# Gated linear attention inside a two-block model: the gate product in one visit on three row quarters, the state products two token tiles at a time

## The reference, cut to what matters

```
gq, gk, gv, gr, glr, fq, fk, fv, ff = split(xn @ w_in[i])
log_a = log_sigmoid(glr @ w_alpha_up[i] + b_alpha[i]) / 16   # glr: (L, 16), log_a: (L, 256)
# chunks: 16 meta tokens, then 8 chunks of 64 tokens
log_b = cumsum(log_a) within a chunk
u_c   = sum_s (k_s * exp(log_end - log_b_s)) v_s^T           # per head 64 x 128
S_c   = exp(log_end_c) * S_{c-1} + u_c
o_t   = q_t^T S_c
```

## Time and profile before

| | us |
|---|---|
| median of 3 runs | 2226.08 (2225.97 to 2226.41) |
| the profiled execution | 2226.62 |
| its span, first to last instruction | 2225.4 |
| PE busy | 2203.2 (99%) |
| DVE, ACT, POOL busy | 1410.5, 1049.4, 119.3 |

### The profile page before, as it was taken

One profiled execution on the slowest core, in us unless ns is written; L12 is line 12 of the kernel. 1 busy time (PEld: TensorE's weight loads), 2 busy tenths in 40 slices (PEclk: granted clock), 3 DMA queues, 4 the chain that ended last, 5 costly groups with the idle time before them and its releaser, 6 DMA issues.

```text
span 2225.4 us, 39293 instructions
## 1 busy us (share of the span) xinstructions
PE 2203.2 (99%) x15807; PEld 2019.1 (91%) x15807; DVE 1410.5 (63%) x2601; ACT 1049.4 (47%) x1947; POOL 119.3 (5%) x203
## 2 busy tenths in 40 slices
PE   9999999999999999999999999999999999999998
PEld 7799999999997899999899888978899888998997
DVE  5356676759743466767689566869455465863664
ACT  5356544347533466543377443223244444552652
POOL 3000010000000001100000010101000000000001
PEclk9999999999999999999999999999999999999999
DMA  6655677345434446642365272768721122543651
GB/s 215 171 128 150 184 185 201 102 143 176 135 93 128 116 131 149 180 118 89 121 173 163 91 180 83 194 176 222 205 72 65 63 97 89 156 159 117 183 170 51
DMA packets 97112, 313.01 MB, mean 141 GB/s; under 512 B 13810, under 2 KB 17812, under 8 KB 95908
## 3 DMA queue, kind: packets, MB, share of 16 engines
q1 hardware_dynamic: 84628, 220.93, 30.8%
q0 software_dynamic: 11584, 88.25, 17.4%
q10 hardware_dynamic: 720, 1.31, 0.2%
HBM read 308.32 MB, written 86.02 MB: 177 GB/s over the span
## 4 chain that ended last, share of the span: by engine, by line
PE 93%; DVE 4%; ACT 2%; issue 1%; DMA 0%; POOL 0%; SPq 0%; ACTq 0%; DVEq 0%; POOLq 0%
PE G L1452 58%; PE G L1489 15%; PE G L1568 7%; PE X L1489 3%; PE X L1788 1%; PE X L1875 1%; PE X L1740 1%; PE X L1764 1%; DVE wL L2465 1%; ACT wH L1928 1%; PE X L1859 1%; PE X L1528 1%; PE X L1844 1%; PE X L1452 1%; PE X L1831 0%
## 5 line engine op out<-in xcount | busy, mean ns | idle before, releaser
L1928 ACT ACTIVATE wH<-raw 128x512 fp32r<-128x512 f32 (+3 forms) x693 | 475.0, 705 | 459.6 <-PE G L1452 381.1
L2465 DVE TENSOR_TENSOR wL<-raw,wH 128x512 fp32r<-128x512 f32 (+3 forms) x693 | 537.8, 788 | 216.4 <-ACT wH L1928 213.5
L1452 PE MATMUL G<-aH,wH 128*128 128x264 f32 (+2 forms) x2000 | 497.2, 314 | 2.4 <-DVE aL L2478 1.7
L1452 PE MATMUL G<-aH,wL 128*128 128x264 f32 (+2 forms) x2000 | 478.9, 305 | 0.0
L1452 PE MATMUL G<-aL,wH 128*128 128x264 f32 (+2 forms) x2000 | 478.8, 304 | 0.0
L1452 PEld LDWEIGHTS G<-aH,wH 128*128 128x128 f32 x2000 | 324.2, 188 | 22.3 <-DVE aL L2478 2.1
L1452 PEld LDWEIGHTS G<-aH,wL 128*128 128x128 f32 x2000 | 322.4, 188 | 16.2
L1452 PEld LDWEIGHTS G<-aL,wH 128*128 128x128 f32 x2000 | 322.7, 188 | 13.1 <-issue 0.2
L1489 PE MATMUL G<-seven,wH 128*128 128x256 f32 (+2 forms) x960 | 177.4, 284 | 1.8 <-DVE wL L2465 1.7
L2624 DVE TENSOR_TENSOR hT<-G,hT 128x528 f32<-128x528 f32 (+1 forms) x83 | 58.0, 699 | 170.3 <-PE G L1452 170.1
L1489 PEld LDWEIGHTS G<-seven,wH 128*128 128x128 f32 x960 | 148.2, 189 | 3.9 <-issue 3.0
(11 more groups left out here) (412 smaller groups left out, 3898.7 us busy)
## 6 DMA issues: line engine op xcount, KB each, us to landing
raw<-weights SPq DMA_DIRECT2D x195, 512.0 KB, 4.1
weight_sums<-weights POOLq DMA_DIRECT2D x72, 704.0 KB, 6.5
raw<-weight_sums SPq DMA_DIRECT2D x160, 256.0 KB, 2.9
raw<-weights SPq DMA_DIRECT2D x48, 704.0 KB, 4.2
raw<-weights SPq DMA_DIRECT2D x121, 256.0 KB, 2.9
weight_sums<-weight_sums POOLq DMA_DIRECT2D x24, 704.0 KB, 5.2
weight_sums<-weights POOLq DMA_DIRECT2D x24, 448.0 KB, 5.1
raw<-weights SPq DMA_DIRECT2D x12, 384.0 KB, 7.5
```

The lines of the kernel that those rows point to most:

```text
L1452: done = e.matmul(m.pair(i)[0:M, bank, 0:n], a[:, k, 0:M], b[:, kx, lo - t0:lo - t0 + n], start=(k == 0 and c == 0), stop=(k == nk - 1 and ...
L1928: e.activation(m.high(i)[:, c], m.raw(i)[:, c], ACT.Copy).then_inc(s.w_hi, 1)
L2465: e.tensor_tensor(m.low(i)[:, c], m.raw(i)[:, c], m.high(i)[:, c].bitcast(F32), ALU.subtract).then_inc(s.w_lo, 1)
```

## The change

The gate product of all five token tiles is made in one step `gz`, and the ACT and DVE chains that used to stand in the three `gz` steps are now three steps `gla` at the old places. For this the low-rank rows exist three times, in row quarters 32, 64 and 96 of `glrT`, and so do the weights `wau`: `sel` has 112 columns, DVE scales three copies, POOL fills ones in rows 32 to 127, and SP issues three loads in place of one. Block 0 uses quarter 96, block 1 quarter 32, block 2 quarter 64; the meta block is computed 128 tokens wide. The state increments are made for token tiles 0 and 1, 2 and 3, and 4, in three visits; two tiles share a bank, side by side. The visits are three background steps apart in place of two.

```diff
             step("fsum", l)
             yield
+            step("gz", l)
             for bk in range(3):
-                step("gz", l, bk)
+                step("gla", l, bk)
                 yield
...
-            for c in range(5):
+            for c in (0, 2, 4):
                 step("gst", l, c)
+                yield
                 yield
                 yield
...
-        self.sel = sb("sel", [128, 48])
+        self.sel = sb("sel", [128, 112])
...
-            self.glrT = sb("glrT", [64, L], F32, c)
+            self.glrT = sb("glrT", [128, L], F32, c)
...
-                self.wau = sb("wau", [49, 256], F32, cf)
+                self.wau = sb("wau", [113, 256], F32, cf)
...
-            done = e.matmul(m.pair(i)[0:48, bank, 0:n], m.sel[:, :], m.osq[:, lo:lo + n], start=True, stop=True)
+            done = e.matmul(m.pair(i)[0:112, bank, 0:n], m.sel[:, :], m.osq[:, lo:lo + n], start=True, stop=True)
...
-    def gz(l, bk):
-        if bk == 0:
-            e.wait_ge(s.psum, NTH["evac", AT["gq", l, 1]])
-            e.wait_ge(s.alpha, 16 * (l + 1))
-        if bk == 2:
-            e.wait_ge(s.rtok, RTOK["attn", l])
-        mt = TOK[BLOCKS[bk][0]][1]
-        for q, j in enumerate(BLOCKS[bk]):
-            t0 = TOK[j][0]
-            done = e.matmul(X[0:mt, bk, 256 * q:256 * q + 256], m.glrT[32:49, t0:t0 + mt], m.wau[32:49, :],
+    def gz(l):
+
+        e.wait_ge(s.psum, NTH["evac", AT["gq", l, 1]])
+        e.wait_ge(s.alpha, 48 * (l + 1))
+        e.wait_ge(s.rtok, RTOK["attn", l])
+        e.wait_ge(s.kzero, l + 1)
+        for bk, q in (0, 0), (1, 0), (2, 0), (1, 1), (2, 1):
+            t0, g = TOK[BLOCKS[bk][q]][0], (96, 32, 64)[bk]
+            done = e.matmul(X[:, bk, 256 * q:256 * q + 256], m.glrT[g:g + 17, t0:t0 + 128], m.wau[g:g + 17, :],
                             start=True, stop=True)
-        done.then_inc(s.gz, 1)
+            if q == len(BLOCKS[bk]) - 1:
+                done.then_inc(s.gz, 1)
...
-        e.wait_ge(s.kd, 3 * l + (1 if c == 0 else 2 if c < 3 else 3))
-        for pr in range(2):
...
+        e.wait_ge(s.kd, 3 * l + (2 if c < 2 else 3))
+        for d in range(c, min(c + 2, 5)):
+            for pr in range(2):
+                for hh in range(2):
+                    q = slice(64 * hh, 64 * hh + 64)
+                    for hf in range(2 if d else 1):
+                        r, at = slice(64 * hf, 64 * hf + 64) if d else slice(0, 16), 256 * (d % 2) + 128 * pr
+                        done = e.matmul(X[q, hf, at:at + 128], m.gk[r, d, 128 * pr + 64 * hh:128 * pr + 64 * hh + 64],
+                                        m.gv[r, d, 256 * pr + 128 * hh:256 * pr + 128 * hh + 128], start=True, stop=True)
...
             scaled(i, m.ffT[:, :], slice(0, 8)).then_inc(*own.one())
-            scaled(i, m.glrT[32:48, :], slice(32, 48)).then_inc(s.psum, 1)
+            for g in (32, 64):
+                scaled(i, m.glrT[g:g + 16, :], slice(g, g + 16)).then_inc(*own.one())
+            scaled(i, m.glrT[96:112, :], slice(96, 112)).then_inc(s.psum, 1)
...
     def gst(l, c):
-        e.wait_ge(s.gst, 18 * l + (4 * c + 2 if c else 2))
+        end = min(c + 2, 5)
+        e.wait_ge(s.gst, 18 * l + 4 * end - 2)
+        for d in range(c, end):
+            state(l, d)
...
         constant(m.glrT[32:64, :], 1.0)
+        constant(m.glrT[64:128, :], 1.0)
...
-        for c, n, row in (0, 8, 0), (32, 16, 8):
+        for c, n, row in (0, 8, 0), (32, 16, 8), (64, 16, 8), (96, 16, 8):
...
-    e.dma_start(m.wau[32:49, :], WAU[0]).then_inc(s.alpha, 16)
+    for g in (32, 64, 96):
+        e.dma_start(m.wau[g:g + 17, :], WAU[0]).then_inc(s.alpha, 16)
```

More of the change, by code:

```diff
@@ L1670, in gst @@
             e.wait_ge(s.state, 9 * l + 2 * c - 1)
-        e.wait_ge(s.kd, 3 * l + (1 if c == 0 else 2 if c < 3 else 3))
-        for pr in range(2):
[L1673 to L1680, removed]
+        e.wait_ge(s.kd, 3 * l + (2 if c < 2 else 3))
[7 more added lines that the diff above has]
+                                        m.gv[r, d, 256 * pr + 128 * hh:256 * pr + 128 * hh + 128], start=True, stop=True)
+                        if pr:
+                            done.then_inc(s.gst, 1)
     def go(l, v):
@@ L2262, in attin, with gla @@
         operand_high(m.q2H[:, h, :] if h < 2 else m.aH[:, h, NM:L], m.attnT[:, h, :], 1.0)
-    def gz(l, bk):
+    def gla(l, bk):
         n = 3 * l + bk + 1
@@ L2400, in act_program @@
     parts = {"high7": high7, "p1st": p1st, "p5th": p5th, "u2nd": u2nd, "c21": c21, "conv7": conv7, "silu7": silu7, "hidh7": hidh7, "split": split, "prep": prep, "xm": xm, "gains": gains, "ffc": ffc, "sq": sq, "rms": rms, "prepmid": prepmid, "last": last, "rmshalf": rmshalf, "rmsmid": rmsmid, "rmsend": rmsend, "midln": midln, "midexp": midexp,
-             "tmout": tmout, "rest": rest, "evac": evac, "mixin": mixin, "attin": attin, "gz": gz, "gb": gb, "gdec": gdec,
+             "tmout": tmout, "rest": rest, "evac": evac, "mixin": mixin, "attin": attin, "gla": gla, "gb": gb, "gdec": gdec,
              "go": go, "gn": gn, "fsum": fsum, "ft": ft, "fs": fs, "fo": fo, "nsq": nsq, "nsum": nsum, "is": iscore, "dt": dt,
@@ L2905, in gst, with state @@
     def gst(l, c):
-        e.wait_ge(s.gst, 18 * l + (4 * c + 2 if c else 2))
+        end = min(c + 2, 5)
+        e.wait_ge(s.gst, 18 * l + 4 * end - 2)
+        for d in range(c, end):
+            state(l, d)
+    def state(l, c):
         if c == 0:
@@ L2917, in gst @@
                 done = e.scalar_tensor_tensor(out=m.S[:, n, pr, :], in0=m.S[:, n - 1, pr, :], scalar=m.dec[:, pr, n - 1:n],
-                                              in1=X[:, hf, 128 * pr:128 * pr + 128], op0=ALU.mult, op1=ALU.add)
+                                              in1=X[:, hf, 256 * (c % 2) + 128 * pr:256 * (c % 2) + 128 * pr + 128],
+                                              op0=ALU.mult, op1=ALU.add)
                 if pr:
@@ L3077, in dve_program @@
              "rmsmid": rmsmid, "midln": midln, "rtok": rtok, "tmout": tmout, "evac": evac, "rest": rest, "normed": normed, "last": last, "store": store,
-             "pads": pads, "gz": gz, "gb": gb, "gst": gst, "gn": gn, "fsum": fsum, "fs": fs, "fmeta": fmeta, "fn": fn, "ftail": ftail,
+             "pads": pads, "gla": gla, "gb": gb, "gst": gst, "gn": gn, "fsum": fsum, "fs": fs, "fmeta": fmeta, "fn": fn, "ftail": ftail,
              "iw": iw, "is": iscore, "itri": itri, "top": top, "mask": mask, "dt": dt, "ds": ds, "dn": dn}
@@ L3207, in pool_program @@
                                    compare_op=ALU.not_equal, fill=1.0, base=-row, pattern=[[-1, n]], channel_multiplier=1)
-            if (t, c) == (3, 32):
+            if (t, c) == (3, 96):
                 done.then_inc(s.sel, 1)
@@ L3247, in zeros @@
             e.wait_ge(s.chunk, AT["seven", 0, 1, 10, 4] + 1)
-            e.dma_start(m.wau[32:49, :], WAU[1]).then_inc(s.alpha, 16)
+            for g in (32, 64, 96):
+                e.dma_start(m.wau[g:g + 17, :], WAU[1]).then_inc(s.alpha, 16)
     def store(half, j):
```

## The result

The changed kernel takes 2222.26 us (median of 20 runs, 2221.86 to 2222.85), the kernel before 2226.22 in the same rounds (20 runs, 2225.83 to 2227.50). The ratio is 0.9982, with a 95% interval of 0.9977 to 0.9988: 3.96 us or 0.18% less, where 4.9 us and 0.22% were forecast. The time lies in the stated range of 2220.1 to 2224.0, but above the forecast's own range of 2220.4 to 2221.7, at the place of rival (b). The gain is within 0.2%: the prediction gave that a chance of 0.34, and 0.62 to more than 0.2%.

What follows compares the result with a forecast made beforehand. PE, busy for 99% of the span, was taken to bound the kernel. Savings of 2 x (1.77 + 0.36 + 0.32) = 4.9 us off the median of 2226.08 gave 2221.2, 0.22% faster, with a range of 2220.1 to 2224.0.

Steps and rivals of the forecast that it cites:

- rival (b): Quarters run at once, but a just-in-time hand-over fails or `ffsel` keeps its price: 0.5 to 2 us lost; chance 0.25.
- Part 1, the gate product: Three `gz` visits (3.05 us) become one of five matmuls on three row quarters (1.28): gain 1.77 a layer.
- (a): In the gate product the quarters run one after another: gain only 2.2 us, time 2223.8; chance 0.08.
- (c): In the gate product each change of quarter empties the array: 4.05 against 3.05 us, time 2226.7; chance 0.03.
- Part 2, the state products: Five state visits (3.78 us a layer) become three (3.42): gain 0.36 a layer.
- the bound without it: First state visit with no change of tiling counted: the added set costs 0.44, not 0.60, gain 0.52 a layer.
- Part 3, the selector: At 112 columns `ffsel` no longer runs in a 64-column tile: gain 0.32 a layer, 0 if still a tile.
- Part 4: Work added elsewhere, DVE copies, POOL selects and memset, SP issues: all taken as covered and priced at 0.
- The other thin hand-over, the bank at 40.5: Layer 0: the bank for the first `gv` product is emptied at 40.5, PE reaches it at 40.8; priced at 0.
- Rival (d): The merge does nothing, because something taken as covered, such as `kzero`, now sets PE's time; chance 0.02.
- first of its two signs of being wrong: The prediction is wrong if the attention stages together give back less than 4.4 us.
- the second: The prediction is wrong if a stage without any edit changes its length.

Runs made afterwards that it cites:

- beside: The changed kernel with the gate product and two of the three state visits moved directly behind meta rows: 2221.03 us (0.9978).
- states: The kernel before with only the state visits merged, three in place of five: 2225.66 us (0.9997).
- wide: The kernel before with only the selector widened to 112 columns, the added ones zero: 2225.53 us (0.9997).
- serial: The changed kernel with all five gate products on one row quarter, the other copies still made and loaded: 2225.57 us (0.9996).

## Why the prediction was right in its mechanism and 0.94 short

**Part 1, the gate product: right.** The visit has 1.07 for a forecast of "about 1.08", and layer 1 gained 1.77, to the hundredth. That is a product of concurrency, as assumed: 2.35 on one quarter, near the 2.41 of its upper bound (2.61 without the 0.20). Rivals (a) and (c) are out: neither 2.4 nor 4 was seen. The 0.20 for leaving the whole array and coming back is confirmed from another side by `beside`, at 0.26 for each adjacency. That it is the array's tiling which is left and come back to is the reading of these rows; what they show is the time.

**Part 2, the state products: mis-sized.** The sum gave 0.36 a layer; the traces give 0.26 and 0.23, and `states` by itself 0.58 for both layers. The visits' own rows are as forecast (1.18, 1.03 and 0.60), and with 1.18 in the first visit the change from 16-row to 64-row tiles did cost like a set of its own (0.58 + 0.60). This is the case with a drain at a change of tiling mode, as the Trainium skill has it (TensorEngine Tiling (Array Packing), Key Properties), and not the bound without it. What was mis-sized is the block behind: the sum took 0.228 a product and 0.20 over for every block. By the same measure the blocks behind the visits of 1.18 and 1.03 have 0.23 over (4.33 and 7.07), and the one behind the meta rows at 76.64, which had a visit directly behind them in the kernel before and now stand alone, has 0.25 (2.99). The row for that was there: in the kernel before, the chain behind the meta rows that stand alone at 92.21 reads

```profile
93.21 2.99 PE G L1568 x12
```

Together 0.03 + 0.03 + 0.05 = 0.11, the missing 0.1 of a layer. What all three have in common is the pace of 0.231 to 0.232 for 10 or 11 products and not 6; DVE's reads are not in it.

**Part 3, the selector: right**, at 0.32 a layer, and `wide` shows that 112 columns are treated as the whole array.

**Part 4, priced at 0: wrong twice, by little.** The split ended at 35.84 for a forecast 35.71, and TensorE lost 0.17, within the "0.2 if it slips". Here "just in time" was a row to be priced, not a zero. The other thin hand-over, the bank at 40.5, held: the block behind the gate product is no longer than in layer 1 once the wait for the split is gone. The GpSimd estimate was the worse one: 20.9 for the fill that DVE wants at 26, "5 us of cover or more". The timeline of POOL in the changed kernel, against the earlier trace rows:

```profile
6.41 8.69 POOL L3218 TENSOR_SCALAR_AFFINE_SELECT sel<-sel 32x8 f32<-32x8 f32 x16
15.20 8.47 POOL L3123 TENSOR_SCALAR xm<-hT,vec 128x32 f32<-128x32 f32 x8
23.73 1.13 POOL L3109 MEMSET glrT<- 32x528 f32 x2
24.91 0.53 POOL L3147 MEMSET fv<- 128x512 f32 x1
```

The selects took 1.3 more than 16 times the mean of before, and the eight `xm`, not touched by the change, 8.47 and not the 5.11 of the kernel before: they had been shifted to where DVE adds squares and splits weights from SBUF to SBUF. There was hardly any cover left: 25.44 against 25.75, and in six of nine profiled executions with this order of GpSimd's work DVE waited, 0.27 to 0.73. That it does not show in the median is luck: the fill comes late only where DVE was early. Rival (d) had named this wait and priced it at a chance of 0.02.

**The sum.** 4.9 was forecast. Missing in the traces are 0.34 at 921 us, 0.17 at the split, 0.23 at the state products and 0.08 at the start; 0.19 came on top, hardly from the change. That makes 0.63 of the 4.9 missing between the spans. The rest of the 0.94, 0.3 to 0.4, is that the profiled execution of before lay 0.40 above its median and the changed one 0.03: the sum took what its rows gave off the median in full. Where in the execution that time went can't be told from one profile. The step at 921 us is the largest that has a place, and was in no part of the prediction: another number of DVE instructions put a late start onto the path. By the first of its two signs of being wrong the prediction holds (the attention stages gave 0.64 + 3.37 + 0.49 = 4.50, and 4.4 was the least), by the second it does not: a stage without any edit changed its length. The forecast stood only 0.4 us outside the bound, and so a loss of 0.94 sufficed to put it within. That is rival (b)'s outcome and time (2221.7 to 2223.2), but only a fifth of the shortfall is rival (b)'s mechanism.

## What to carry to other kernels

Price a small visit by how deep its matmuls stand on each part of the array, plus about 0.2 us for leaving the full array, and put visits next to each other to pay that once. A hand-over with a margin under the spread of the start is a cost, and it also swallows whatever is saved ahead of it: here TensorE stood still for 0.56 ahead of a late split, and kept 0.11 of a lead of 0.60, until the late engine was relieved. Work shifted in time is not work unchanged: where a shifted GpSimd group lands beside DVE, take its duration from rows with DVE beside it. And when a kernel this tight moves by 0.3 us at a place that no edit touches, count instructions before looking for a reason in the work.

## What the runs showed that I had not expected

- An engine can start an instruction 0.28 us (ACT) or 0.35 us (DVE) later than usual at fixed places of its instruction order, whatever stands there: in all 14 traces on records that are a multiple of 128 plus 63. In the changed kernel these are 1343, 1599 and 1983 of ACT and 1343 of DVE. They repeat in every kernel that has as many instructions before them, and move when four idle waits are inserted. The page of the changed kernel lists two queues that carry instructions, 126 packets with 2.06 MB and 54 with 0.44 MB (16 KB and 8 KB each):

```profile
q8 instruction: 126, 2.06, 0.4%
...
q14 instruction: 54, 0.44, 0.1%
```

  Behind each of the 47 late starts a packet of q14 starts within 0.6 to 4.1 us, where its 54 packets are some 41 us apart on average. That the late starts are block boundaries of this loading is an inference from that and from the 128; no run here changes the loading to show it. Why most places of this kind are not late stays open.
- GpSimd's `xm` (one multiplication, 128 x 32) takes 0.36 us alone and 0.60 to 0.63 beside DVE's `aL` operations in the kernel before, and up to 1.28 in the changed kernel, where DVE's additions and weight splits (two SBUF inputs as well) run beside it; the fills, which read nothing, take 0.53 to 0.58 in both, in the kernel before beside such DVE operations. The Trainium skill gives the reason (SBUF — State Buffer, SBUF: two separate sides): DVE operations with two SBUF inputs and GpSimd operations that read SBUF take turns on a shared port pair, and one waits for the whole of the other. The rows agree, down to the fills being spared; why `aL` costs `xm` less than the others do, they don't tell.
- A granted clock of 0.50 for 2.6 us at the start in `serial`, in a stretch where the changed kernel has 1.00, shown above.
- Two edits outside the change, visits side by side and the copies on ACT, give 2219.52 (2219.43 with the fills first): 6.6 us or 0.3% below the kernel before, against the change's 3.96.
